# Two token-mixing stages reordered: turned blocks under the projection, gate sigmoids in the attention passes, results in pairs

## The chip, the cores and the metric

The program runs on one core of a Trainium2 chip. The metric is the time of one execution on the device in microseconds (us). The engines are TensorE (matrix products and transposes), VectorE, ScalarE, GpSimd and the DMA queues; each works through its own instructions in order, and they wait for each other by semaphores.

## The reference

The reference is two blocks one behind the other on 256 tokens of width 1024. The second block, where the change is, has two layers of feed-forward, token mixing, feed-forward. The mixing, cut to what matters:

```python
proj = n @ w_in                     # 3072 columns of q, k, v and small gates, then 3 x 1024 merge gates
y_a = _nsa_attention(...)           # 4 heads: compressed, selected, window
y_b = _dilated_attention(...)       # 3 groups of 2 heads, mixed by softmax over the groups' log-sum-exp
y_c = _forgetting_attention(...)    # 6 heads, bias cumsum(log_sigmoid(f_logit + f_bias))
g_a, g_b, g_c = jnp.split(jax.nn.sigmoid(merge_g), 3, axis=-1)
merged = g_a * (y_a @ br_nsa) + g_b * (y_b @ br_dil) + g_c * (y_c @ br_fox)
return merged @ w_out
```

## The kernel before, in words

All matrix products run in fp32 by three multiplications each: operands are split into a high part (fp32r) and the rest, and `mm3` (L353 to L355) multiplies high by high, low by high and high by low. Weights come in units of 128x2048 (1 MB) through a ring of three slots. For each unit ScalarE writes the high half (`conv_hi`, L274) once TensorE has used the unit three before, and VectorE then the low half (`conv_lo`, L280), at which TensorE may start; the queue of loads (L245) refills a slot when its low half is made. Where these conversions stand in the three engines' orders is written out by hand, and nothing is reordered by a planner.

A mixing stage (`pe_layer`, `act_layer`, `dve_layer`) has four parts. The projection is 12 units of 48 multiplications; ScalarE copies each result into `qj` (L1988). In layer 0 VectorE also does 16 steps of a modulation sum there (L320, L326), whose inputs share the load queue. In the second part come three of the twelve merge-gate units (`gate_unit`), the rotation of q and k (six VectorE instructions, L813 to L819), the forget gate's logarithm, 17 blocks of 128 columns turned by 34 transposes (L1851) and copied into `tb` by ScalarE (L2008) and VectorE (L2137) in turn, and the compression (two units of small multiplications). The third part is 20 attention passes of two query tiles each. In pass i TensorE makes the scores, turns the weights of pass i-1 and multiplies those of pass i-2 with v; VectorE takes the negated row maximum (L2229), ScalarE the exponentials with their sums (L2040) and a copy of the turned weights (L2051). Seven gate units (5 to 11) fill the gaps in halves: two passes of three have one, and in the third pass ScalarE copies the gate out and converts a unit, VectorE makes its low half. `oc_part` (L2201) is the compressed branch's output ahead of pass 0. In the fourth part the groups' weights are computed with a logarithm (L2054) and an exponential (L2056), the twelve gates get their sigmoid on ScalarE (L2060), outputs are normalised (L2261 to L2272) and turned (L421), split into halves (L469, L475), multiplied with the three branch matrices, gated (L2280), added (L2284), turned and split again, and multiplied with the output matrix.

Of the kernel before, what the change touches and what calls it, by code (L numbers as in the profile page):

```python
# [70 lines left out]
NTB = len(T_COLS)  # L71

# [51 lines left out]
def bass_network(nc, W, AD, x_in, ctx_in, s1_in, s2_in, k1_in, masks_in, gf_in, out):  # L124
    with ExitStack() as ctx:
# [1621 lines left out]
        def final_norm(dve, k, t, dst, done):  # L1747
# [8 lines left out]
                 "hid_made": 1, "ck_mm": 1, "ck_out": 1, "cs_mm": 1, "cs_sub": 1, "zeroed": 1, "hid_turned": 1, "hid_act": 1, "oc_out": 1, "sig_done": 3, "y_half": 1, "cs_exp": 1, "cs_done": 1, "cp_mm": 1,  # L1756
                 "cp_out": 1, "oc_mm": 1, "s2_mm": 20, "negmax2": 20, "exp2": 20, "p2_turned": 20, "pt2_out": 20, "pv2": 20,
                 "ya_done": 1, "den_ln": 1, "lse_sub": 1, "lse_exp": 1, "m_out": 12, "y2_turned": 7, "y2_hi": 7,
                 "y2_lo": 7, "dil_mm": 1, "br_out": 3, "y2_made": 1}
# [3 lines left out]
        ORDER2 = list(range(11, 17)) + list(range(11))  # L1763
# [15 lines left out]
        nsa_part = [tbf[:, 6 * S:8 * S], tbf[:, 8 * S:10 * S]]  # L1779
        dil_part = [tbf[:, b * S:b * S + S] for b in (2, 3, 4)]  # L1780
# [32 lines left out]
        def pe_layer(pe, l):  # L1813
# [12 lines left out]
            gate_pe(pe, N2, 1, l, 2)  # L1826
            for j in range(3, 12):
                pe.wait_ge(*B["q_out"].at(j - 3, l))
                project(unit(pe, QK0 + j, E0), hhi, hlo, QB[j % 3]).then_inc(unit_used, 1)
                if l == 0 and j in (6, 10):  # L1830
                    half_sum(pe, QKV_HALVES[j // 10], 3)
# [6 lines left out]

            gate_unit(0, 4)
            pe.wait_ge(*B["q_out"].at(11, l))  # L1840
            if l == 0:
                pe.wait_ge(*ada_out.at(QKV_HALVES[1] - PE_HALVES))
            pe.wait_ge(*N2.row.at(1, l))
            for i, b in enumerate(ORDER2):
                if i == 6:
                    gate_unit(1, 5)
                    pe.wait_ge(*B["rope2"].at(0, l))
                if i >= 4:
                    pe.wait_ge(*(B["tb_act"] if i % 2 == 0 else B["tb_dve"]).at(i // 2 - 2, l))
                for t in range(NT):  # L1850
                    ins = nc.tensor.transpose(PS[:, i % 4, t * P:(t + 1) * P], qj[:, t, T_COLS[b]:T_COLS[b] + P], ident)  # L1851
                ins.then_inc(*B["tb_mm"].up)
            gate_unit(2, 6)

# [15 lines left out]
            pe.wait_ge(*B["cum_out"].at(0, l))  # L1870
            for t in range(NT):
                ins = nc.tensor.transpose(PS[:, 3, (1 + t) * P:(2 + t) * P], ct[:, t], ident)
            ins.then_inc(*B["cum_turned"].up)
# [71 lines left out]
            pe.wait_ge(*B["y2_made"].at(0, l))  # L1945
            turn(pe, B["y2_turned"], xn, 0, 6)
            pe.wait_ge(*B["y2_lo"].at(2, l))

            u = unit(pe, BR0, E0)
            for kk in range(2):  # L1950
                ins = rows_product(u, kk, hhi[:, kk], hlo[:, kk], 4, kk == 0, kk == 1)
            ins.then_inc(unit_used, 1)
            u = unit(pe, BR0 + 1, E0)
            rows_product(u, 0, hhi[:, 2], hlo[:, 2], 0, True, True).then_inc(*B["dil_mm"].up)
            pe.wait_ge(*B["br_out"].at(0, l))
            rows_product(u, 1, hhi[:, 3], hlo[:, 3], 4, True, False).then_inc(unit_used, 1)
            u = unit(pe, BR0 + 2, E0)
            for kk in range(2):
                ins = rows_product(u, kk, hhi[:, 4 + kk], hlo[:, 4 + kk], 4, False, kk == 1)
            ins.then_inc(unit_used, 1)  # L1960
            pe.wait_ge(*B["br_out"].at(2, l))
            turn(pe, B["y2_turned"], mg, 0, DC)
# [11 lines left out]
        def act_layer(act, l):  # L1974
# [8 lines left out]
            norm_act(act, N2, 1, l, shift2(1, l), QK0, E0, x2_at(1, l))  # L1983
            for j in range(12):
                if j == 3:
                    gate_act(act, N2, 1, l, 2)
                act.wait_ge(unit_used, E0 * 3 + (QK0 + j + 1))
                nc.scalar.activation(qj[:, :, j * 256:j * 256 + 256], PS[:, QB[j % 3]].rearrange("p (t n) -> p t n", t=2),  # L1988
                                     ACT.Copy).then_inc(*B["q_out"].up)
                conv_hi(act, QK0 + j + RING, E0)  # L1990

            def gate_out(f, bank, conv=True):

                act.wait_ge(unit_used, E0 * 3 + (CG[f] + 1))
                nc.scalar.activation(G[f], PS[:, bank].rearrange("p (t n) -> p t n", t=2), ACT.Copy).then_inc(*B["m_out"].up)
                if conv:
                    conv_hi(act, CG[f] + RING, E0)

            act.wait_ge(*B["fox_abs"].at(0, l))
            nc.scalar.activation(ge.rearrange("p (t n) -> p t n", t=2), qj[:, :, C_G:C_F], ACT.Exp, scale=-1.0)  # L2000
            nc.scalar.activation(fe, fe, ACT.Exp, scale=-1.0)
            act.drain()
            nc.scalar.activation(fe, fe, ACT.Ln, bias=1.0).then_inc(*B["fox_ln"].up)
            def turned_out(a, b):
                for i in range(a, b, 2):
# [545 lines left out]
```

## Time and profile before

| | us |
|---|---|
| median of 3 runs | 2143.99 (2140.99 to 2145.86) |
| profiled execution, its own time | 2144.57 |
| its span, first to last instruction | 2142.8 |
| granted TensorE clock, mean | 0.949 of full |
| TensorE busy | 92% of the span |

The profile is of one execution. Layer 0's mixing stage begins its projection some 905 us behind the start, layer 1's some 727 us later. A multiplication's busy time overlaps with the next one's, so lengths of stretches are more telling than sums of durations.

### The profile page before, as it was taken

How to read it: one execution, taken by the hardware profiler on the slowest of the kernel's cores; microseconds unless marked ns; L12 is line 12 of the kernel's file. 1: busy time of each engine (PE TensorE's matmuls, PEld its weight loads, DVE VectorE, ACT ScalarE, POOL GpSimd, SP SyncE). 2: the span in 40 equal slices, each digit the busy share in tenths (PEclk: the TensorE clock that was granted, in tenths of full speed). 3: DMA queues.
4: the chain of work that ended last, by engine and by line, in shares of the span. 5: the costliest groups of instructions: out<-in, count | busy, mean ns of one | idle time of the engine just before them, and what ended most of it. 6: DMA issues, size and time to landing. Idle time of an engine off the chain costs nothing.

```text
span 2142.8 us, 29870 instructions
## 1 busy us (share of the span) xinstructions
PE 1964.4 (92%) x12658; PEld 1746.6 (82%) x12658; DVE 1377.5 (64%) x1467; ACT 997.1 (47%) x1161; POOL 82.3 (4%) x105
## 2 busy tenths in 40 slices
PE   7999879999997999997997899999999879879998
PEld 3977668888885999896875799989998877768997
DVE  4888558999995777664335587777755443355444
ACT  3344337777774433443444433343334434435342
POOL 1320000000001000000000000000001000000000
PEclk9988979999998999997998999999999989989999
DMA  8655328999994687553321387658753432124554
GB/s 347 238 210 185 156 109 334 367 357 350 349 376 173 256 299 262 224 217 107 109 79 71 146 325 293 266 190 335 292 185 139 176 118 79 67 91 158 178 194 149
DMA packets 63877, 458.42 MB, mean 214 GB/s; under 512 B 7040, under 2 KB 7296, under 8 KB 8832
## 3 DMA queue, kind: packets, MB, share of 16 engines
q1 hardware_dynamic: 63744, 456.51, 56.7%
q8 instruction: 100, 1.64, 0.3%
q14 instruction: 33, 0.27, 0.0%
HBM read 455.43 MB, written 1.05 MB: 213 GB/s over the span
## 4 chain that ended last, share of the span: by engine, by line
issue 80%; PE 7%; DVE 6%; DMA 3%; ACT 2%; POOL 1%; DVEq 1%; POOLq 0%; ACTq 0%; SPq 0%
DMA ada<-in_ada 2%; DVE acc L326 2%; PE PS L353 2%; PE PS L354 2%; PE PS L355 1%; DVE wlo L280 1%; PE PS L1194 1%; POOL Z L485 1%; ACT whi L274 1%; DVE hlo L462 1%; PE PS L1258 1%; DMA raw<-in_stream 0%; ACT Z L441 0%; PE PS L1270 0%; DVE sm L1702 0%
## 5 line engine op out<-in xcount | busy, mean ns | idle before, releaser
L280 DVE TENSOR_TENSOR wlo<-raw,whi 128x2048 fp32r<-128x2048 f32 x282 | 646.6, 2294 | 409.1 <-ACT whi L274 403.6
L274 ACT ACTIVATE whi<-raw 128x2048 fp32r<-128x2048 f32 x282 | 538.5, 1913 | 408.4 <-PE PS L355 364.1
L353 PE MATMUL PS<-whi,hhi 128*128 128x256 f32 (+1 forms) x1616 | 530.2, 328 | 39.7 <-DVE wlo L280 11.7
L354 PE MATMUL PS<-wlo,hhi 128*128 128x256 f32 (+1 forms) x1616 | 518.5, 321 | 0.0
L355 PE MATMUL PS<-whi,hlo 128*128 128x256 f32 (+1 forms) x1616 | 518.0, 321 | 0.0
L353 PEld LDWEIGHTS PS<-whi,hhi 128*128 128x128 f32 x1616 | 319.9, 198 | 65.8 <-issue 13.7
L355 PEld LDWEIGHTS PS<-whi,hlo 128*128 128x128 f32 x1616 | 319.6, 198 | 19.2
L354 PEld LDWEIGHTS PS<-wlo,hhi 128*128 128x128 f32 x1616 | 320.3, 198 | 17.6
L353 PE MATMUL PS<-hhi,whi 128*128 128x256 f32 x1152 | 326.6, 284 | 2.2 <-DVE mod L348 2.2
L355 PE MATMUL PS<-hhi,wlo 128*128 128x256 f32 x1152 | 326.0, 283 | 0.0
L354 PE MATMUL PS<-hlo,whi 128*128 128x256 f32 x1152 | 326.0, 283 | 0.0
L353 PE MATMUL PS<-whi,zr 128*128 128x512 f32 (+2 forms) x624 | 232.0, 375 | 13.9 <-DVE zr L2159 11.1
L326 DVE SCALAR_TENSOR_TENSOR acc<-ada,cs,acc 128x512 f32<-128x512 f32 x308 | 236.8, 769 | 8.9
L355 PE MATMUL PS<-whi,zr 128*128 128x512 f32 (+2 forms) x624 | 227.4, 367 | 0.0
L354 PE MATMUL PS<-wlo,zr 128*128 128x512 f32 (+2 forms) x624 | 227.1, 367 | 0.0
L353 PEld LDWEIGHTS PS<-hhi,whi 128*128 128x128 f32 x1152 | 221.0, 192 | 4.6 <-DVE mod L348 3.5
L354 PEld LDWEIGHTS PS<-hlo,whi 128*128 128x128 f32 x1152 | 221.0, 192 | 1.1
L355 PEld LDWEIGHTS PS<-hhi,wlo 128*128 128x128 f32 x1152 | 221.0, 192 | 0.0
L353 PEld LDWEIGHTS PS<-whi,zr 128*128 128x128 f32 (+1 forms) x624 | 113.7, 182 | 35.0 <-DVE zr L2159 11.2
L355 PEld LDWEIGHTS PS<-whi,zr 128*128 128x128 f32 (+1 forms) x624 | 113.5, 182 | 20.8
L354 PEld LDWEIGHTS PS<-wlo,zr 128*128 128x128 f32 (+1 forms) x624 | 113.7, 182 | 18.9
L280 DVE TENSOR_TENSOR wlo<-ada,whi 128x2048 fp32r<-128x2048 f32 x48 | 109.9, 2291 | 12.0 <-ACT whi L274 12.0
(377 smaller groups left out, 1822.0 us busy)
## 6 DMA issues: line engine op xcount, KB each, us to landing
raw<-in_stream SPq DMA_DIRECT2D x285, 1024.0 KB, 4.8
ada<-in_ada SPq DMA_DIRECT2D x92, 1024.0 KB, 4.9
ada<-in_stream SPq DMA_DIRECT2D x48, 1024.0 KB, 4.9
raw<-in_ada SPq DMA_DIRECT2D x3, 1024.0 KB, 15.5
xs<-in_x SPq DMA_DIRECT2D x1, 1024.0 KB, 11.7
Z<-in_ada SPq DMA_DIRECT2D x1, 1024.0 KB, 19.4
Z<-in_ctx SPq DMA_DIRECT2D x1, 1024.0 KB, 11.8
masks<-in_masks SPq DMA_DIRECT2D x2, 512.0 KB, 9.6
```

The costliest lines, as they stand in the source:

```text
L274: nc.scalar.activation(whi[:, s], src, ACT.Copy).then_inc(hi_ready, 1)
L280: nc.vector.tensor_tensor(wlo[:, s], src, whi[:, s].bitcast(F32), ALU.subtract).then_inc(lo_ready, 1)
L326: ins = nc.vector.scalar_tensor_tensor(a, w, c, a, ALU.mult, ALU.add)
L353: nc.tensor.matmul(out_, ah, bh, start=start, stop=False, skip_group_check=check)
L354: nc.tensor.matmul(out_, ah, bl, start=False, stop=False, skip_group_check=check)
L355: return nc.tensor.matmul(out_, al, bh, start=False, stop=stop, skip_group_check=check)
L462: nc.vector.tensor_tensor(lo[:, 4 * b:4 * b + 4, t * P:(t + 1) * P], ntmp[:, 4 * b:4 * b + 4], hi[:, 4 * b:4 * b + 4, t * P:(t + 1) * P].b ...
L485: nc.gpsimd.tensor_tensor(diag, mid(ident, [P, DC, P]), bc(gcol[:, :], [P, DC, P]), ALU.mult).then_inc(*N.diag.up)
L1194: ins = nc.tensor.matmul(PS[0:2, bank, :], cs[:, n:16:8], slot[:, 512 * k:512 * k + 512], start=n == 0, stop=n == 7)
L1258: ins = nc.tensor.matmul(PS[:, i % 2], q, k, start=True, stop=i >= 16, skip_group_check=i < 16)
```

## The change

In both layers: the last of the 12 projection units (small gates, values of the dilated group) goes first, so the forget gate is computed under the projection; the rotation follows VectorE's conversion of step 5; the 17 blocks are turned in five portions behind projection units 7 to 11, in an order that puts the compressed keys first, through result banks 2 to 5. `oc_part` goes ahead of a conversion. The merge gates are computed as 1/(1 + exp(-x)): gates 0 to 3 by an exponential in passes 0 to 3, gates 4 to 11 by one at their copy, then an addition and a reciprocal on VectorE; eleven of these fall in the passes, the twelfth behind. The groups' weights are computed from maxima and sums without a logarithm, in passes 15 to 18, and the outputs are normalised, turned and split in three pairs; the first two already beside the last passes. The halves of these pairs have places of their own (`zr`), and the branch products use other banks. The third branch's result is gated and merged in quarters, each turned as it is made. The products themselves, their number and the units' number stay the same; units are only reordered in the weight stream. Comment lines in the cut diff name the engine.

```diff
+QKV_ORDER = [11] + list(range(11))
+TURNS_AT = {7: (0, 4), 8: (4, 8), 9: (8, 12), 10: (12, 16), 11: (16, 17)}
...
-        ORDER2 = list(range(11, 17)) + list(range(11))
+        ORDER2 = [10, 8, 9, 6, 7, 0, 1, 2, 3, 4, 5] + list(range(11, 17))
...
# TensorE, pe_layer
+            def turn_blocks(a, b):
+                for i in range(a, b):
+                    if i >= 4:
+                        pe.wait_ge(*(B["tb_act"] if i % 2 == 0 else B["tb_dve"]).at(i // 2 - 2, l))
+                    for t in range(NT):
+                        c = T_COLS[ORDER2[i]]
+                        ins = nc.tensor.transpose(PS[:, 2 + i % 4, t * P:(t + 1) * P], qj[:, t, c:c + P], ident)
+                    ins.then_inc(*B["tb_mm"].up)
             for j in range(3, 12):
                 pe.wait_ge(*B["q_out"].at(j - 3, l))
                 project(unit(pe, QK0 + j, E0), hhi, hlo, QB[j % 3]).then_inc(unit_used, 1)
...
+                if j == 7:
+                    pe.wait_ge(*B["rope2"].at(0, l))
+                    pe.wait_ge(*N2.row.at(1, l))
+                if j in TURNS_AT:
+                    pe.wait_ge(*B["q_out"].at(j - 1, l))
+                    turn_blocks(*TURNS_AT[j])
...
             gate_unit(0, 4)
-            for i, b in enumerate(ORDER2):
-                if i == 6:
-                    gate_unit(1, 5)
-                    pe.wait_ge(*B["rope2"].at(0, l))
...
+            gate_unit(1, 5)
+            pe.wait_ge(*B["cum_out"].at(0, l))
+            for t in range(NT):
+                ins = nc.tensor.transpose(PS[:, 3, (1 + t) * P:(2 + t) * P], ct[:, t], ident)
+            gate_unit(2, 6)
...
+                if i == PASSES2:
+                    pe.wait_ge(*B["y2_made"].at(0, l))
+                    turn_two(xn, 0, 6)
+            pe.wait_ge(*B["y2_made"].at(1, l))
+            turn_two(xn, 2, 4)
+            pe.wait_ge(*B["y2_lo"].at(0, l))
+            rows_product(u, 0, yb_hi[:, 0], yb_lo[:, 0], 0, True, False)
+            pe.wait_ge(*B["y2_made"].at(2, l))
+            turn_two(xn, 4, 5)
+            rows_product(u, 1, yb_hi[:, 1], yb_lo[:, 1], 0, False, True).then_inc(unit_used, 1)
...
+            for j in range(4):
+                pe.wait_ge(*B["br_out"].at(2 + j, l))
+                turn_two(mg, 2 * j, 4 + j)
# ScalarE, act_layer: gate_out of units 4 and up writes exp(-x); in the passes
+                    if i < 4:
+                        nc.scalar.activation(G[i], G[i], ACT.Exp, scale=-1.0).then_inc(*B["gate_exp"].up)
+                    if i == 17:
+                        act.wait_ge(*B["lse_sub"].at(0, l))
+                        nc.scalar.activation(lw, lw, ACT.Exp).then_inc(*B["lse_exp"].up)
...
-            nc.scalar.activation(lnd, den2[:, 16:28], ACT.Ln).then_inc(*B["den_ln"].up)
-            for b in range(3):
-                for f in range(4 * b, 4 * b + 4):
-                    ins = nc.scalar.activation(G[f], G[f], ACT.Sigmoid)
# VectorE, dve_layer, under the projection
             for j in range(12):
                 conv_lo(dve, QK0 + j + RING, E0)
+                if j == 2:
+                    fox_start()
+                if j == 4:
+                    fox_log()
+                if j == 5:
+                    rotate()
...
                     half_step(dve, v, n)
                     half_step(dve, v, n + 1)
+                if j in TURNS_AT:
+                    turned_out(*TURNS_AT[j])
...
-            conv_lo(dve, CG[4] + RING, E0)
             nc.vector.tensor_tensor(oc_part...).then_inc(*B["oc_out"].up)
+            conv_lo(dve, CG[4] + RING, E0)
+            def gate_sigmoid(f):
+                dve.wait_ge(*(B["gate_exp"] if f < 4 else B["m_out"]).at(f, l))
+                nc.vector.tensor_scalar(G[f], G[f], 1.0, None, ALU.add)
+                dve.drain()
+                nc.vector.reciprocal(G[f], G[f])
...
                 if done[1]:
                     conv_lo(dve, CG[done[0]] + RING, E0)
+                    gate_sigmoid(done[0])
+                if i < 5:
+                    gate_sigmoid(i)
+                if i == 15:
+                    dil_weights()
+                if i == 18:
+                    dil_out()
+                if i == 19:
+                    fox_out(14, 2, 4, 256)
+            fox_out(16, 4, 5, 0)
+            split_lo(0, 6, yb_hi[:, 0:2], yb_lo[:, 0:2])
+            split_lo(1, 4, yb_hi[:, 2:4], yb_lo[:, 2:4])
+            split_lo(2, 5, yb_hi[:, 4:6], yb_lo[:, 4:6])
             conv_lo(dve, CG[11] + RING, E0)
+            gate_sigmoid(11)
...
+            for j in range(4):
+                ins = gated(0, j, 0, mg)
+            ins.then_inc(*B["br_out"].up)
             conv_lo(dve, BR0 + RING, E0)
+            for j in range(4):
+                gated(1, j, 4, mt2[0])
+            nc.vector.tensor_tensor(mg, mg, mt2[0], ALU.add).then_inc(*B["br_out"].up)
+            for j in range(2):
+                for t in range(NT):
+                    c = slice(256 * j, 256 * j + 256)
+                    nc.vector.tensor_tensor(mt2[1][:, t, c], PS[:, 2 * t, c], G[8 + j][:, t], ALU.mult)
+            merged(0)
+            gated(2, 2, 0, mt2[1])
+            merged(1)
+            gated(2, 3, 0, mt2[1])
+            merged(2)
+            merged(3)
+            for j in range(4):
+                split_lo(3 + j, 4 + j, hhi[:, 2 * j:2 * j + 2], hlo[:, 2 * j:2 * j + 2])
+            for u in range(1, 3):
+                conv_lo(dve, BR0 + u + RING, E0)
```

## Rows read from the trace of the kernel before

**Rows 1.** The page, part 1: busy us of each engine, share of the span, instructions.
```profile
PE 1964.4 (92%) x12658; PEld 1746.6 (82%) x12658; DVE 1377.5 (64%) x1467; ACT 997.1 (47%) x1161; POOL 82.3 (4%) x105
```

**Rows 2.** Stretches: length; busy us (instructions) of PE, PEld, DVE, ACT, POOL; clock, DMA, GB/s.
```profile
924.60:930.30 5.70, 5.70 (x50) 5.70 (x49) 3.05 (x3) 2.40 (x2) 0.00 (x0) 1.00 0.52 185
...
972.40:1023.70 51.30, 35.26 (x283) 34.06 (x281) 20.65 (x34) 18.45 (x24) 0.00 (x0) 0.77 0.28 101
...
1016.40:1020.80 4.40, 4.40 (x49) 4.40 (x50) 0.00 (x0) 0.00 (x0) 0.00 (x0) 0.61 0.58 227
...
1020.80:1023.70 2.90, 2.90 (x52) 2.90 (x49) 0.70 (x1) 1.91 (x1) 0.00 (x0) 1.00 0.00 0
...
1042.20:1142.20 100.00, 94.92 (x640) 79.00 (x640) 32.78 (x36) 40.89 (x114) 0.00 (x0) 0.97 0.22 74
...
1142.20:1185.30 43.10, 24.69 (x100) 20.12 (x100) 29.33 (x40) 21.03 (x28) 0.00 (x0) 0.80 0.24 86
...
1699.60:1750.80 51.20, 35.23 (x287) 34.03 (x286) 20.54 (x33) 18.45 (x24) 0.00 (x0) 0.77 0.28 103
```

**Rows 3.** Timeline of TensorE: start, us, instruction, count, [idle before, releaser].
```profile
978.20 1.03 PE L1851 MATMUL PS<-k,Z 128*128 128x128 f32 x8
...
984.62 0.69 PE L1851 MATMUL PS<-k,Z 128*128 128x128 f32 x2 [5.39 <-ACT Z L2008]
...
1000.35 2.82 PE L1851 MATMUL PS<-k,Z 128*128 128x128 f32 x12 [1.95 <-DVE Z L2137]
...
1016.39 0.32 PE L353 MATMUL PS<-whi,zr 128*32 128x128 f32 x1 [5.54 <-DVE zr L2159]
```

**Rows 4.** Timeline of ScalarE and VectorE in layer 0's projection, and the rotation.
```profile
944.03 1.91 ACT L274 ACTIVATE whi<-raw 128x2048 fp32r<-128x2048 f32 x1 [7.13 <-DMA raw<-in_stream]
...
945.98 2.29 DVE L280 TENSOR_TENSOR wlo<-raw,whi 128x2048 fp32r<-128x2048 f32 x1 [9.26 <-ACT whi L274]
...
977.35 0.48 DVE L813 TENSOR_TENSOR xn<-Z,k 128x320 f32<-128x320 f32 x1
...
979.52 0.49 DVE L819 TENSOR_TENSOR Z<-xn 128x320 f32<-128x320 f32 x1
```

**Rows 5.** Timeline of one block of three passes (a maximum comes first).
```profile
1069.74 0.69 DVE L2229 TENSOR_REDUCE sm<-PS 128x2 f32<-128x512 f32 x1 [5.38 <-PE PS L1915]
...
1072.13 1.93 ACT L274 ACTIVATE whi<-raw 128x2048 fp32r<-128x2048 f32 x1
...
1074.09 2.29 DVE L280 TENSOR_TENSOR wlo<-raw,whi 128x2048 fp32r<-128x2048 f32 x1 [3.65 <-ACT whi L274]
...
1076.30 0.69 DVE L2229 TENSOR_REDUCE sm<-PS 128x2 f32<-128x512 f32 x1
...
1077.98 0.55 PE L1924 MATMUL PS<-k,ada 128*128 128x128 f32 x3 [0.80 <-ACT ada L2040]
```

**Rows 6.** VectorE's instructions by line and shape: count, busy us, mean ns.
```profile
L320 DVE TENSOR_SCALAR acc<-ada,cs 128x512 f32<-128x512 f32 x44 | 23.0, 523 | 11.0 <-DMA ada<-in_ada 11.0
...
L2219 DVE TENSOR_TENSOR Z<-Z 128x512 f32<-128x512 f32 x2 | 1.4, 693 | 0.2
...
L2129 DVE RECIPROCAL sm<-sm 128x24 f32<-128x24 f32 x2 | 0.6, 303 | 0.1
...
L2192 DVE RECIPROCAL acc<-acc 128x8 f32<-128x8 f32 x2 | 0.4, 204 | 0.1
...
L1169 DVE RECIPROCAL sm<-sm 128x2 f32<-128x2 f32 x1 | 0.2, 168 | 0.1
```

**Rows 7.** Timeline behind the passes, TensorE and VectorE.
```profile
1150.73 2.82 PE L421 MATMUL PS<-k,xn 128*128 128x128 f32 x12 [8.56 <-DVE xn L2272]
...
1163.88 2.48 DVE L2280 TENSOR_TENSOR Z<-PS,Z 128x512 f32<-128x512 f32 x4 [7.32 <-PE PS L355]
...
1171.03 2.29 DVE L2284 TENSOR_TENSOR Z<-Z,ada 128x2048 f32<-128x2048 f32 x1
...
1180.34 3.57 PE L421 MATMUL PS<-k,Z 128*128 128x128 f32 x16 [5.43 <-DVE Z L2284]
```

More of the change, by code:

```diff
@@ L1944, in pe_layer @@
                     gate_unit(f, 7, tile)
[L1945 to L1946 removed]
+                if i == PASSES2:
[4 more added lines that the diff above has]
+            pe.wait_ge(*B["y2_lo"].at(0, l))
+            u = unit(pe, BR0, E0)
+            rows_product(u, 0, yb_hi[:, 0], yb_lo[:, 0], 0, True, False)
@@ L1955, in pe_layer @@
             pe.wait_ge(*B["br_out"].at(0, l))
-            rows_product(u, 1, hhi[:, 3], hlo[:, 3], 4, True, False).then_inc(unit_used, 1)
+            rows_product(u, 1, yb_hi[:, 3], yb_lo[:, 3], 0, True, False).then_inc(unit_used, 1)
             u = unit(pe, BR0 + 2, E0)
[L1958 to L1962, printed above, removed]
+            rows_product(u, 0, yb_hi[:, 4], yb_lo[:, 4], 0, False, False)
@@ new lines, in pe_layer @@
+            wh, wl = (w.rearrange("p (k n) -> p k n", k=2)[:, 1] for w in u)
+            for half in range(2):
+                for t in range(NT):
+                    o, w = slice(t * P, (t + 1) * P), slice(half * 512, half * 512 + 512)
+                    ins = mm3(PS[:, 2 * t + half], yb_hi[:, 5, o], yb_lo[:, 5, o], wh[:, w], wl[:, w], False, True)
+                ins.then_inc(*(unit_used, 1) if half else B["dil_mm"].up)
+            for j in range(4):
+                pe.wait_ge(*B["br_out"].at(2 + j, l))
+                turn_two(mg, 2 * j, 4 + j)
@@ L1999, in act_layer @@
[L1999 to L2005, printed above, removed]
-                    act.wait_ge(*B["tb_mm"].at(i, l))
-                    k = ORDER2[i]
-                    nc.scalar.activation(tb[:, k], PS[:, i % 4, 0:256], ACT.Copy,
-                                         scale=HD ** -0.5 if k in T_SCALED else 1.0).then_inc(*B["tb_act"].up)
@@ L2012, in act_layer @@
-            conv_hi(act, CG[0] + RING, E0)
-            turned_out(0, 6)
-            conv_hi(act, CG[1] + RING, E0)
-            turned_out(6, NTB)
-            for f in range(2):
-                gate_out(f, 4 + f, False)
-            gate_out(2, 6)
+                if j == 3:
+                    act.wait_ge(*B["fox_abs"].at(0, l))
+                    nc.scalar.activation(ge.rearrange("p (t n) -> p t n", t=2), qj[:, :, C_G:C_F], ACT.Exp, scale=-1.0)
+                    nc.scalar.activation(fe, fe, ACT.Exp, scale=-1.0)
+                    act.drain()
+                    nc.scalar.activation(fe, fe, ACT.Ln, bias=1.0).then_inc(*B["fox_ln"].up)
@@ L2296, in dve_layer, with merged @@
-            split_dve(dve, B["y2_hi"], B["y2_lo"], 3, 4, l)
+            for j in range(4):
+                gated(1, j, 4, mt2[0])
+            dve.drain()
+            nc.vector.tensor_tensor(mg, mg, mt2[0], ALU.add).then_inc(*B["br_out"].up)
+            dve.wait_ge(*B["dil_mm"].at(1, l))
+            def merged(j):
+                c = slice(256 * j, 256 * j + 256)
+                nc.vector.tensor_tensor(mg[:, :, c], mg[:, :, c], mt2[1][:, :, c], ALU.add).then_inc(*B["br_out"].up)
+            for j in range(2):
+                for t in range(NT):
+                    c = slice(256 * j, 256 * j + 256)
+                    nc.vector.tensor_tensor(mt2[1][:, t, c], PS[:, 2 * t, c], G[8 + j][:, t], ALU.mult)
@@ L2297, in dve_layer @@
+            dve.drain()
+            merged(0)
+            dve.wait_ge(unit_used, E0 * 3 + (BR0 + 3))
+            gated(2, 2, 0, mt2[1])
+            merged(1)
+            gated(2, 3, 0, mt2[1])
+            dve.drain()
+            merged(2)
+            merged(3)
+            for j in range(4):
+                split_lo(3 + j, 4 + j, hhi[:, 2 * j:2 * j + 2], hlo[:, 2 * j:2 * j + 2])
+            for u in range(1, 3):
+                conv_lo(dve, BR0 + u + RING, E0)
             conv_lo(dve, WO0 + RING, E0)
```

259 lines of the change are left out of this document (137 added, 122 removed).

## The prediction

> **What bounds the kernel now.** I read the shares of the engines first: TensorE is busy for 1964 of 2143 us, VectorE for 64%, ScalarE for 47% [rows 1]. So in most stretches a change is worth what it does to TensorE's queue, and only idle or slow-clock TensorE time can be won. The table by stretches shows where that is in a mixing stage. In the projection TensorE never rests: 50 multiplications take 5.7 us, so a unit of 48 takes about 5.8. The 51.3 us behind it (first gate unit, turns, compression) hold only 35 us of TensorE work, at a mean granted clock of 0.77 of full; the 43.1 us behind the passes hold 25, at 0.80. The 100 us of passes are 95% busy. The other layer repeats this to 0.1 us [rows 2]. In the turns TensorE stands still for 5.4 us until the last projected unit has been copied and rotated, later again, the last time for 2.0 us, and for 5.5 us ahead of the compression [rows 3]. Behind the passes it waits 8.6 us for weights, mixing and turning inputs, and 5.4 us for the merged result [rows 7]. All of that is what the change attacks. What it gives away lies in the passes.
>
> **Turns under the projection: a gain of 22.9 us per layer.** Old: 51.3 us [rows 2]. New: 34 turns (8 take some 0.9 us net [rows 3]) 4.1 us; three gate units at 5.8, 17.4 us; two compression units at 2.9 us, as the one at full clock took [rows 2], 5.8 us; the small products and the turned sums 1.1 us. Sum 28.4, gain 22.9. It needs each operand early. The units' low halves follow a unit's end by 0.6 + 1.9 + 2.3 = 4.8 us and are wanted 11.5 us behind it; ScalarE does 0.6 + 1.9 + 2 x 0.4 and VectorE 2.3 + 2 x 0.4 us per unit of 6.7, so both keep up. The forget gate's exponentials and logarithm fall in one such unit, where ScalarE's 3.3 us leave as much idle. At the compression the operand (ready about 11.5 us behind the start of the first gate unit) is long there when TensorE comes to it at 18.4. What is late behind it, the activation of the hidden row, keeps its order and its delay.
>
> **Layer 0 gives back 5.7 us.** There VectorE also does 16 steps of modulation, and a weight unit lands late: its conversion starts at 944.03 after a wait of 7.1 us on the DMA, and its low half ends at 948.27 [rows 4], with a quarter of a us to spare before TensorE's next unit. The transfer waits for the modulation step behind which the change puts the 0.8 us of the forget gate, so it lands later by 0.8. Then come the low half (949.1) and the six rotation instructions, 2.7 us from 977.35 to 980.01 [rows 4], now ahead of everything: the first turns wait until 951.9, 2.3 to 3.4 us behind the place where TensorE is ready; the modulation steps behind them (1.5 us each unit) make VectorE's first copy late too, at 961.5, so the next turns wait 2.5 us (or the slow clock of the first wait takes the same time). Together 5.7. Without this queue in layer 1: nothing.
>
> **Gates in the passes: the price of a reciprocal.** Twelve sigmoids on ScalarE behind the passes become exponentials there plus, on VectorE, an addition (about 0.5 us, as the 128x512 instruction with a factor, mean 523 ns [rows 6]) and a reciprocal over 128x512. The trace has none of that size. Its bounds: an ordinary instruction of 512 elements, 0.69 us; and the slope of the small reciprocals, 168 ns for 2 elements, 204 for 8, 303 for 24 [rows 6]: (303 - 168)/22 = 6.1 ns per element, so 0.16 + 512 x 6.1 = 3.3 us. The slope is even over all sizes, while ordinary instructions cost (2290 - 693)/1536 = 1.04 ns [rows 4, 6]. I take 3.3; with the addition and the drain between, a gate costs VectorE 3.86 us. The upper bound is eight ordinary passes per element, 8 x 1.04 x 512 = 4.3 us.
>
> The Trainium skill, VectorE: DVE Perf Modes, under "First, the fixed hardware budget", says that a reciprocal is an iterative divide with a repeat count of 8. The trace agrees in kind, at six ordinary elements' time rather than eight. It speaks against this change; by eight, each sigmoid would cost 1 us more, and that case is a rival below.
>
> Is VectorE's time hidden? It has 67 idle us in the 100 [rows 2], and 11 sigmoids are 42 us: yes by the share, no by the order. A block of three passes takes 13.6 us. Its chain: maximum at 1069.74, exponentials, gate copy, copy of the turned block, conversion on ScalarE from 1072.13, low half on VectorE from 1074.09, and only then the next pass's maximum at 1076.30, whose exponential TensorE awaits for 0.8 us already [rows 5]. So there is no slack: the sigmoid of 3.86 us goes between low half and maximum, and the whole of it is TensorE's wait, 0.8 becoming 4.7 us. Four blocks (maxima of passes 9, 12, 15, 18) give 4 x 3.86 = 15.4 us. The first two blocks carry five more sigmoids. I walk them: oc_part now ends at 1042.95, conversion 1045.3, maximum 0 1046.0, gate exponential 0.6 and pass 0.9, sigmoid 0 until 1050.5, maximum 1 1051.2, sigmoid 1 until 1055.7, maximum 2 1056.4, exponentials and the three ScalarE pieces until 1061.0, low half 1063.3, sigmoids 5 and 2 until 1071.0, exponential 3 ready at 1073.3 (before: 1064.4). The same walk through sigmoids 3, 4 and 6 gives exponential 6 at 1093.3 instead of 1077.9: +15.4 us. The 1.9 us that oc_part wins by going ahead of a conversion are inside that. Sum 30.8 us per layer. The dilated group's weights and outputs (3 us at passes 15 and 18) lie beside gate work or in the last wait.
>
> To this comes the clock. A wait of 5.5 us left the clock at 1.2 GHz: 49 multiplications in 4.4 us where 52 then took 2.9 [rows 2, 3], so a wait costs some 1.5 us again. The 0.8 us waits of the passes leave it full (0.97 [rows 2]). Five to six waits of 4.7 to 9.5 us, and TensorE's next gate half is in the chain: 7.5 us (bounds 0 and 12). The Trainium skill, TensorE: Matmul & The Clock Gate, in "Part 1", says that the throttled state is the default and activity releases it; this agrees with those rows. Passes: +38.3 us per layer.
>
> **Behind the passes: a gain of 10.7 us per layer.** Removed: logarithm, two table loads, all but one sigmoid, the dilated mixing. New, from the last pass's end (0): last outputs 1.05, low half of the first pair 2.4, first product (12 multiplications of 512, 2.8 us) to 5.1, turn, second to 8.4, third to 11.2. VectorE meanwhile: low halves to 7.0, conversion 9.3, last sigmoid 13.2, four gated products of 2.48 us in all [rows 7] 15.7. TensorE waits for these 4.5 us and runs on partly at the slow clock: 19.8, 22.6, 25.4. VectorE: conversion, second branch 2.48, addition 2.29 [rows 7] to 22.9, then four halves and the merging in quarters to 29.8, four low halves 32.4. The output product starts at 32.4 instead of 43.1. The splitting into pairs helps little, because VectorE is last at every step.
>
> **The sum.** Per layer -22.9 + 38.3 - 10.7 = +4.7; two layers +9.4; with layer 0's 5.7, +15.1 us. The profiled execution took 2144.57 us (span 2142.8), 0.6 above the median 2143.99; 2144.6 + 15.1 = 2159.7, against the median 2159.
>
> **The rivals.**
> Cheap reciprocal (faster). If the 512-element reciprocal costs like any other, 0.69 us, a gate costs 1.25 us, the passes +7 us (+14 if the 2.1 us waits slow the clock), the tail gains 13.5: per layer -29 to -22, in all 2092 to 2106, say 2100. It decides from where a reciprocal is under about 2.6 us: at 3.86 us for a gate the change loses 4.7 a layer, each 0.1 us less returns 1.1. For it: no large reciprocal is in the trace. Against it: five sizes on one line. 0.17.
> Clock stays up (no change). Waits of 4.7 us broken by multiplications don't bring the clock down: 7.5 us and 1.4 in the tail back per layer, 2142. For it: the waits are shorter than the 5.5 us that brought it down, and multiplications stand between them. Against: the first stretch behind the passes, at 0.80 with waits of that size. 0.14.
> The turns stall the projection in both layers (slower). Each of the five stops waits 2.0 us for copies, as the last turns did before [rows 3], +10 us a layer: 2159.7 + 20 = 2180. Against: each copy has a unit of 5.8 us. 0.07.
> Eight passes per element (slower): +1 us per sigmoid, eleven in the chain, 2183. 0.05.
>
> **How the numbers follow.** My forecast has 0.57, with a range of its own of 2143 to 2177 (clock 0 to 12, walk within 3 us a layer, layer 0's wait 2 to 9). What this measurement can tell is 0.2%, 4.3 us. Slower: 0.57 x 0.92 + 0.12 = 0.64. Same: 0.57 x 0.05 + 0.14 x 0.6 = 0.11. Faster: the rest, 0.25. The range goes from 2110, which leaves out most of the cheap reciprocal, to 2180.
>
> **What would show it.** The row of the reciprocal over 128x512 on VectorE, at 3.3 us or not: it decides most. TensorE's wait ahead of the turned blocks in the passes, 4.7 us instead of 0.8, some six times a layer, and the clock there; the stretch of passes at 138 us instead of 100. Gate unit 0 to the second compression unit in 24 us, with no wait of over 1 us. In layer 0 a wait of 2 to 3 us on the rotation. From the passes' end to the output product 32 us, with VectorE last. I am wrong if the passes stay within 115 us, or if the front's 22.9 us turn up as waits in the projection.

## The result, and the profile after

The changed kernel takes 2154.51 us (median of five runs, 2153.53 to 2156.53) against 2143.95 (2140.99 to 2145.86) for the kernel before: ratio 1.0051, 95% interval [1.0037, 1.0065]. It is slower by 10.6 us; 2159 was predicted. The profiled spans are 2154.8 and 2142.8 us. Here the differences are told by stage, cut at the same events in both traces (us, after minus before; layer 0 and layer 1):

```
stage                                        before        after         difference     predicted
projection to end of compression         104.8, 102.4   86.0,  79.4   -18.8, -23.0   -17.2, -22.9
compression to first scores               18.3,  18.3   18.3,  18.3     0.0,   0.0
passes, to the last value product        100.0,  99.9  139.9, 136.4   +39.9, +36.5   +38.3
behind them, to the output product        43.2,  43.1   32.9,  32.9   -10.3, -10.2   -10.7
```

They sum to +14.1 us; 2.1 us less stand outside the mixing stages, which makes the 12.0 of the spans. The page of after, part 1, answers to [rows 1]: VectorE has 86 us more, TensorE 12 more with the same instructions.

```profile
PE 1976.2 (92%) x12658; PEld 1758.8 (82%) x12658; DVE 1463.1 (68%) x1525; ACT 978.9 (45%) x1137; POOL 82.8 (4%) x105
```

The stretches of after (columns as in [rows 2]): front, passes and tail of layer 0, then of layer 1.

```profile
918.25:1004.27 86.02, 83.13 (x731) 82.68 (x731) 53.65 (x63) 39.10 (x42) 2.93 (x5) 0.98 0.52 191
1022.56:1162.42 139.86, 112.30 (x647) 96.49 (x647) 75.87 (x71) 43.03 (x119) 0.00 (x0) 0.82 0.15 53
1162.42:1195.31 32.89, 22.91 (x96) 17.42 (x95) 25.77 (x33) 9.71 (x11) 0.00 (x0) 0.90 0.18 64
1658.63:1738.05 79.42, 79.42 (x716) 79.41 (x715) 43.10 (x45) 38.77 (x42) 0.00 (x0) 1.00 0.50 180
1756.35:1892.71 136.36, 109.16 (x647) 93.21 (x647) 75.90 (x71) 43.03 (x119) 0.00 (x0) 0.85 0.16 55
1892.71:1925.65 32.94, 22.96 (x96) 17.49 (x94) 25.77 (x33) 9.71 (x11) 0.00 (x0) 0.90 0.18 64
```

Read three things. In layer 1 the front is pure TensorE work: 79.42 busy of 79.42 us at clock 1.00, where the turns had left holes. In the passes TensorE is idle for 27.6 us (139.86 - 112.30) instead of 5.1 [rows 2], and its same work costs 17.4 us more (112.30 against 94.92), since the granted clock is 0.82 instead of 0.97 (of the 17.4, some 0.6 us are the first pair's transposes, which now stand in this stretch). And VectorE has more than twice the work, 75.9 us instead of 32.8.

VectorE's groups by shape show the price (count, busy us, mean ns, idle before). The reciprocal costs the 3.3 us that the small sizes of [rows 6] gave on one line (16 of the 24 instructions of each kind are in this group; the other groups' means are within 6 ns of these):

```profile
L2287 DVE RECIPROCAL Z<-Z 128x512 f32<-128x512 f32 x16 | 53.6, 3353 | 1.2
...
L2285 DVE TENSOR_SCALAR Z<-Z 128x512 f32<-128x512 f32 x16 | 6.6, 414 | 4.2 <-ACT Z L2073 4.2
```

A block of three passes, from the timeline of VectorE and ScalarE, answers to [rows 5]. Between the low half (1083.91) and the next maximum there was nothing before; now addition and reciprocal stand there, and the exponential waits for the maximum behind them:

```profile
1083.91 2.29 DVE L282 TENSOR_TENSOR wlo<-raw,whi 128x2048 fp32r<-128x2048 f32 x1 [3.65 <-ACT whi L276]
1086.11 0.42 DVE L2285 TENSOR_SCALAR Z<-Z 128x512 f32<-128x512 f32 x1
...
1086.61 3.35 DVE L2287 RECIPROCAL Z<-Z 128x512 f32<-128x512 f32 x1
1089.88 1.22 DVE L2333 TENSOR_REDUCE sm<-PS 128x2 f32<-128x512 f32 x2
1090.54 0.37 ACT L2080 ACTIVATE ada<-PS,sm 128x128 f32<-128x128 f32 x1 [6.67 <-DVE sm L2333]
```

The turned blocks are the three transposes of a pass's weights, which TensorE can start only when the pass's exponentials are made. Those of passes 3, 6, 9, 12, 15 and 18 in layer 0 (timeline, idle time before and its releaser in brackets):

```profile
1052.76 0.90 PE L1942 MATMUL PS<-k,ada 128*128 128x128 f32 x3 [7.21 <-ACT ada L2080]
...
1071.88 0.90 PE L1942 MATMUL PS<-k,ada 128*128 128x128 f32 x3 [4.50 <-ACT ada L2080]
...
1091.51 0.90 PE L1942 MATMUL PS<-k,ada 128*128 128x128 f32 x3 [4.50 <-ACT ada L2080]
...
1111.87 0.90 PE L1942 MATMUL PS<-k,ada 128*128 128x128 f32 x3 [4.86 <-ACT ada L2080]
...
1132.96 0.90 PE L1942 MATMUL PS<-k,ada 128*128 128x128 f32 x3 [2.64 <-ACT ada L2080]
...
1153.89 0.90 PE L1942 MATMUL PS<-k,ada 128*128 128x128 f32 x3 [2.73 <-ACT ada L2080]
```

Each takes 0.90 us where the same block took 0.55 before [rows 5]. The three stretches from the second of them on (columns as above) show why: a clock of 0.50 and 0.62, that is mostly the 1.2 GHz level, for 6.6 us behind the wait, then full again.

```profile
1071.88:1073.70 1.82, 1.82 (x9) 1.82 (x10) 0.00 (x0) 1.51 (x6) 0.00 (x0) 0.50 0.00 0
1073.70:1078.50 4.80, 4.80 (x27) 4.64 (x26) 0.00 (x0) 0.00 (x0) 0.00 (x0) 0.62 0.00 0
1078.50:1087.40 8.90, 8.51 (x57) 6.61 (x56) 4.11 (x4) 3.58 (x7) 0.00 (x0) 1.00 0.06 9
```

The same wait doesn't always slow the clock as much. Layer 1 has the same six waits within 0.4 us, but at passes 15 and 18 its turned blocks still take 0.55 us, and the clock falls later and for a shorter time. Pass 15, its block and the two stretches behind the wait (in layer 0 the first 5.5 us behind this wait were at 0.50):

```profile
1865.10 0.55 PE L1942 MATMUL PS<-k,ada 128*128 128x128 f32 x3 [2.64 <-ACT ada L2080]
```

```profile
1865.10:1867.00 1.90, 1.90 (x11) 1.83 (x12) 0.11 (x1) 1.51 (x6) 0.00 (x0) 0.70 0.00 0
1867.00:1872.80 5.80, 5.80 (x33) 4.89 (x31) 0.00 (x0) 0.00 (x0) 0.00 (x0) 0.80 0.00 0
```

### The profile page after: what moved, and what is told of

It reads as the page before. It is cut to its first block, busy times and chain, and to the rows that moved or that the text cites. A ratio compares the mean times of both kernels' runs of the same rounds, so it can differ in the third digit from the quotient of the medians.

```text
span 2154.8 us, 29942 instructions
## 1 busy us (share of the span) xinstructions
PE 1976.2 (92%) x12658; PEld 1758.8 (82%) x12658; DVE 1463.1 (68%) x1525; ACT 978.9 (45%) x1137; POOL 82.8 (4%) x105
## 4 chain that ended last, share of the span: by engine, by line
issue 80%; DVE 6%; PE 6%; DMA 3%; ACT 2%; POOL 1%; DVEq 1%; POOLq 0%; ACTq 0%; SPq 0%
DMA ada<-in_ada 2%; DVE acc L328 2%; DVE wlo L282 2%; PE PS L355 1%; PE PS L356 1%; PE PS L357 1%; ACT whi L276 1%; DMA raw<-in_stream 1%; PE PS L1196 1%; POOL Z L487 1%; DVE hlo L464 1%; PE PS L1260 0%; ACT Z L443 0%; DVE acc L322 0%; DVE Z L459 0%
## 5 line engine op out<-in xcount | busy, mean ns | idle before, releaser
L355 PE MATMUL PS<-whi,hhi 128*128 128x256 f32 (+1 forms) x1568 | 517.7, 330 | 30.9 <-DVE wlo L282 11.9
L356 PE MATMUL PS<-wlo,hhi 128*128 128x256 f32 (+1 forms) x1568 | 504.8, 322 | 0.0
L357 PE MATMUL PS<-whi,hlo 128*128 128x256 f32 (+1 forms) x1568 | 504.1, 321 | 0.0
L355 PE MATMUL PS<-whi,zr 128*128 128x512 f32 (+2 forms) x672 | 250.9, 377 | 15.0 <-DVE Z L2364 8.9
L357 PE MATMUL PS<-whi,zr 128*128 128x512 f32 (+2 forms) x672 | 245.6, 369 | 0.0
L356 PE MATMUL PS<-wlo,zr 128*128 128x512 f32 (+2 forms) x672 | 245.2, 369 | 0.0
L355 PEld LDWEIGHTS PS<-whi,zr 128*128 128x128 f32 (+1 forms) x672 | 122.8, 183 | 39.3 <-DVE Z L2364 9.7
L357 PEld LDWEIGHTS PS<-whi,zr 128*128 128x128 f32 (+1 forms) x672 | 122.4, 182 | 23.3
L356 PEld LDWEIGHTS PS<-wlo,zr 128*128 128x128 f32 (+1 forms) x672 | 122.7, 183 | 21.1
```

The source lines that it names most:

```text
L355: nc.tensor.matmul(out_, ah, bh, start=start, stop=False, skip_group_check=check)
L356: nc.tensor.matmul(out_, ah, bl, start=False, stop=False, skip_group_check=check)
L357: return nc.tensor.matmul(out_, al, bh, start=False, stop=stop, skip_group_check=check)
```

## The experiments

All start from the kernel after unless another is named; ratios are against the kernel before, from the same chip. "Passes" and "tail" are the third and fourth stage of the table, layer 0 and layer 1. The recorded expectations end the passes a little earlier, so the kernel after reads 138.6 and 135.9 us there, and its tails 34.2 and 33.4, where the table has 139.9 and 136.4, and 32.9 twice.

**Without the reciprocal.**

This leaves out the reciprocal, so the gates are wrong. The exponential's factor is made small as well, which keeps them near 2.

```diff
-nc.scalar.activation(G[f], src, ACT.Exp, scale=-1.0)
+nc.scalar.activation(G[f], src, ACT.Exp, scale=-0.001)
...
 def gate_sigmoid(f):
     nc.vector.tensor_scalar(G[f], G[f], 1.0, None, ALU.add)
-    dve.drain()
-    nc.vector.reciprocal(G[f], G[f])
```

> The kernel after, with the reciprocal (and the drain ahead of it) left out of the twelve gate units, so that the gates are 1 + exp(-0.001 x) and not the sigmoid; the addition of 0.42 us, the exponentials and the order of all work stay. Theory (the 3.35 us reciprocal stands between the low half of the gate weights and the next row maximum, and the passes wait for it): the passes of attention fall from 138.6 and 135.9 us back to 102 to 107, the 4.5 us waits of TensorE ahead of every third pass go, its clock stays up, and the whole comes to 2080 to 2092 us. Rival (the exponentials and copies of ScalarE, or a TensorE clock that falls for another reason, stretch the passes): passes stay over 120 us and the whole over 2120. Rival (VectorE catches up behind the passes): passes 105, but the tail grows by over 5 us per layer.

Measured: 2076.63 us, ratio 0.970 [0.969, 0.972]; passes 103.1 and 103.1, tail 28.6 and 28.6, front unchanged. The passes are as the theory said, the whole is 3 us below its range, and both rivals are refuted: this one instruction costs the change some 78 us, 35 of them in each layer's passes and 4.3 in each tail.

**The gate as a hyperbolic tangent.**

```diff
-nc.scalar.activation(G[f], src, ACT.Exp, scale=-1.0)
+nc.scalar.activation(G[f], src, ACT.Tanh, scale=0.5)
...
-nc.vector.tensor_scalar(G[f], G[f], 1.0, None, ALU.add)
-dve.drain()
-nc.vector.reciprocal(G[f], G[f])
+nc.vector.tensor_scalar(G[f], G[f], 0.5, 0.5, ALU.mult, ALU.add)
```

> The kernel after with the gate as 0.5 tanh(x/2) + 0.5: ScalarE computes Tanh where it computed Exp, VectorE one multiply-and-add in place of addition, drain and reciprocal. Theory as for the kernel without reciprocals: VectorE's 3.86 us per gate become about 0.42, passes 102 to 107 us, whole 2080 to 2095 us if Tanh costs what Exp does and no table is loaded between it and the exponentials. Rival (each Tanh between two Exp of the passes loads a table twice, over 1 us each): 11 gate units per layer add two loads, 20 us or more per layer, whole over 2120 us. The Trainium skill, ScalarE: Activation LUTs (Table sets: the hidden batching unit), puts exp and tanh into one set; no run here has shown it so far, and this one does.

Measured: 2078.18 us, ratio 0.970 [0.969, 0.972]; passes 103.0 and 103.0, tail 27.4 and 27.4; the whole is 2 us below the theory's range. No table load stands among the exponentials and hyperbolic tangents of the passes. The Trainium skill (ScalarE: Activation LUTs, Table sets: the hidden batching unit) puts exp and tanh into one set, and this run agrees. ScalarE's Tanh over 128x512 takes 592 to 631 ns (means of its groups), and VectorE's groups show the block shrunk from 3.86 us for addition, drain and reciprocal to 0.42 us:

```profile
L2285 DVE TENSOR_SCALAR Z<-Z 128x512 f32<-128x512 f32 x16 | 6.6, 423 | 4.2 <-ACT Z L2073 4.2
```

**The same sigmoids at other places.**

```diff
+SIGMOIDS_AT = {1: (0,), 3: (1,), 4: (2,), 6: (3,), 7: (4,), 9: (5,), 10: (6,), 13: (7,), 15: (8,), 16: (9,), 19: (10,)}
...
-                    gate_sigmoid(done[0])
-                if i < 5:
-                    gate_sigmoid(i)
+                for f in SIGMOIDS_AT.get(i, ()):
+                    gate_sigmoid(f)
```

> The kernel after with the same eleven sigmoids inside the passes, each put off to a place behind the row maximum of a pass whose filler is a gate half, or behind the last fillers: behind the maxima of passes 1, 3, 4, 6, 7, 9, 10, 13, 15, 16 and 19 in place of 0 to 4, 3, 6, 9, 12, 15 and 18. Nothing is left out. Theory that the order costs the time, not the share of VectorE (it is busy 76 of 138.6 us): one reciprocal of 3.35 us fits beside the 3.1 us gate half, the passes come to 103 to 115 us and the whole to 2090 to 2115. Rival (a block of 3.86 us ahead of any maximum costs nearly itself, as a pass has only two score banks): passes stay at 130 or more and the whole within 10 us of 2154.5.

Measured: 2093.37 us, ratio 0.977 [0.976, 0.979]; passes 103.7 and 103.6, tail 34.9 and 33.8. The stretch of the passes:

```profile
1023.96:1127.65 103.69, 98.87 (x645) 82.73 (x644) 75.19 (x70) 43.35 (x119) 0.00 (x0) 0.93 0.19 72
```

VectorE works 75.2 us as in after, but the stretch is 36 us shorter than layer 0's in after, and TensorE is idle for 4.8 us. So the order was the matter and not the share of VectorE. The eleven blocks of 3.86 us cost 3.7 us over the kernel before when they stand behind a maximum that TensorE follows with a gate half, and 39.9 and 36.5 us, waits and slower clock together, when they stand ahead of the next maximum. Some 2 and 1 us of the gain come back in the tails.

**The clock held up.**

```diff
+FILLS = {3: 52, 15: 20, 18: 20}
...
                     p = i - 1
+                    if p % 3 == 0 and 3 <= p <= 18:
+                        for n in range(FILLS.get(p, 32)):
+                            nc.tensor.matmul(PS[:, 7, 256:512], zb[:, 0:P], zb[:, 0:256], start=True, stop=True)
                     pe.wait_ge(*B["exp2"].at(p, l))
```

> The kernel after with 20 to 52 multiplications of 128x256 (bf16, their result unused, into a free half of a bank) put into each of TensorE's six waits ahead of the turned blocks of passes 3, 6, 9, 12, 15 and 18; all that is computed stays. Theory (7.5 us per layer of the passes are TensorE at its lower clock behind these waits, where a gate half takes 4.1 to 5.2 us in place of 3.1): the gate halves return to 3.1 us, the passes fall by 5 to 8 us per layer and the whole to 2138 to 2146. Rival (VectorE sets the pace of the passes, and TensorE's slower blocks lie in its shadow): under 2 us per layer, 2150 to 2155. Rival (the added multiplications overrun the waits and the clock stays low all the same): 2155 or more.

Measured: 2136.18 us, ratio 0.997 [0.996, 0.998], 18 us under after and even under the kernel before; passes 127.3 and 126.3. The theory's direction holds and its size is too small: the passes are 12.6 and 10.1 us shorter. Both rivals are refuted. The stretches of the passes, both layers:

```profile
1023.89:1151.20 127.31, 120.11 (x835) 100.82 (x835) 75.91 (x71) 43.03 (x119) 0.00 (x0) 0.95 0.16 59
1746.96:1873.27 126.31, 117.41 (x835) 97.86 (x835) 75.76 (x71) 43.06 (x119) 0.00 (x0) 0.97 0.17 59
```

All of VectorE's blocks are still there (75.9 us). So of the 39.9 and 36.5 us at least 12.6 and 10.1 were the clock. The tail of layer 0 is 1.9 us longer than in after (34.8 us): behind its first wait of 1.6 us the clock is at 0.64 for 4.7 us, where after has 1.00.

**The reciprocal kept for units 0 to 4 only**, tanh for 5 to 11 (both edits as above, by `f > 4`).

> The kernel after with the reciprocal kept for gate units 0 to 4 (five blocks of 3.86 us in passes 0 to 4) and 0.5 tanh(x/2) + 0.5 for units 5 to 11. Nothing is left out. Theory (a block costs only where it stands between the low half and the next maximum while nothing is queued on TensorE; in passes 0 to 2 the gate halves of 3.1 us cover most of it, and only pass 3 has a pile of two): passes 106 to 113 us, whole 2085 to 2100. Rival (each of the eleven blocks costs its share of the 36 us alike, five of them 16): passes 118 to 120, whole 2105 to 2112.

Measured: 2086.26 us, ratio 0.974 [0.973, 0.976]; passes 109.1 and 107.4, tail 27.4 and 28.6. Five blocks with the reciprocal cost 6.1 and 4.4 us over the 103.0 of the tanh kernel, which has none, and the eleven cost 36.9 and 33.4: not alike, and the theory holds. (In layer 0, 1.5 of the 6.1 us stand ahead of the first turned block, where TensorE doesn't wait and its clock is lower than in the tanh kernel; a slower clock is part of the price here too.) TensorE's timeline at the turned blocks of passes 3 and 6 shows the pile at the place expected, and little behind it; in after the same two waits were 7.21 and 4.50 us:

```profile
1046.71 0.55 PE L1942 MATMUL PS<-k,ada 128*128 128x128 f32 x3 [3.83 <-ACT ada L2082]
...
1062.47 0.55 PE L1942 MATMUL PS<-k,ada 128*128 128x128 f32 x3 [1.14 <-ACT ada L2082]
```

**Sigmoids behind the passes**, as before the change, with the rest of the change kept.

```diff
-                    ins = nc.scalar.activation(G[f], src, ACT.Exp, scale=-1.0)
+                    ins = nc.scalar.activation(G[f], src, ACT.Copy)
...
-                    gate_sigmoid(done[0])
-                if i < 5:
-                    gate_sigmoid(i)
...
             split_hi(2, 5, yb_hi[:, 4:6])
+            for b in range(3):
+                for f in range(4 * b, 4 * b + 4):
+                    ins = nc.scalar.activation(G[f], G[f], ACT.Sigmoid)
+                ins.then_inc(*B["sig_done"].up)
```

> The kernel after with the gates as in the kernel before: the units are copied as they are, and ScalarE applies Sigmoid to all twelve behind the passes (after the first parts of y are taken out), so that no gate work stands on VectorE in the passes. The turns under the projection, the weights without logarithm, the results in pairs and the new order of the last products stay. Nothing is left out. Theory (all that the change lost is the gate units' place): passes 101 to 104 us, tail 34 to 40 us (twelve Sigmoid of some 0.6 us and a table load in each direction stand ahead of the gated products), front 86.0 and 79.4 us as in after, whole 2088 to 2100 us. Rival (the tail's gain was the sigmoids' and goes with them): tail 43 us or more, whole over 2104.

Measured: 2076.60 us, ratio 0.970 [0.969, 0.971]; passes 98.9 and 98.9, tail 30.8 and 30.8. It comes out better than the theory's numbers: passes 1 us under those before, and a tail 12.3 us shorter although all twelve sigmoids are back in it. ScalarE's timeline there shows why they cost so little:

```profile
1124.71 0.60 ACT L2091 ACTIVATE zr<-PS 128x512 fp32r<-128x512 f32 x1 [3.78 <-PE PS L1864]
1125.33 1.28 ACT L2098 ACT_TABLE_LOAD   x1
1126.62 4.28 ACT L2098 ACTIVATE Z<-Z 128x512 f32<-128x512 f32 x8
```

They run mostly beside TensorE's products of the first branch (1121.2 to 1130.2). So everything in the change but the gates' place and form is worth about 66 us.

**The rotation ahead of its low half.**

```diff
             for j in range(12):
+                if j == 5:
+                    rotate()
                 conv_lo(dve, QK0 + j + RING, E0)
...
-                if j == 4:
+                if j == 4 and l:
                     fox_log()
-                if j == 5:
-                    rotate()
...
                     half_step(dve, v, n + 1)
+                if j == 4 and not l:
+                    fox_log()
```

> The kernel after with the rotation ahead of the low half of its turn in both layers, and, in layer 0, the logarithm's end behind the half steps. Nothing is left out. Theory (in layer 0 TensorE's 2.68 us wait ahead of the first turns under the projection, and the clock at its lower level that follows over unit 8, come from the rotation that stands behind VectorE's half steps): layer 0's part up to the compression falls by 2.7 to 6 us, the whole to 2149 to 2152. Rival (the wait is for q_out or the ring and not for the rotation): no change, 2154 to 2155.

Measured: 2152.90 us, ratio 1.006 [1.004, 1.008], 0.9 us above the theory's range; front of layer 0 82.9 instead of 86.0 us, span 2151.6 instead of 2154.8. By the timed medians the step of 1.6 us is within the noise; the stage in the trace shows the 3.1 us. The wait in after that it removes:

```profile
950.60 1.54 PE L1837 MATMUL PS<-k,Z 128*128 128x128 f32 x8 [2.68 <-DVE Z L821]
```

**Both of the last kind together**, tanh and rotation.

> The kernel after with the gates as 0.5 tanh(x/2) + 0.5 and with the rotation ahead of the low half of its turn, layer 0's logarithm behind the half steps. Nothing is left out. Theory (the two gains stand in different stages and add): front of layer 0 82.9 us, passes 103 us, whole 2074 to 2076 us, 1.5 to 3.5 under the kernel with the tanh alone. Rival (clock or DMA takes the 3.1 us back later): within 1 us of 2078.

Measured: 2075.17 us, ratio 0.969 [0.967, 0.970]; front of layer 0 83.0, passes 102.8 and 103.1, tail 28.6 and 28.6. 3.0 us under tanh alone, as the theory said. In the tails 1.2 us each go back, and the clock takes them. Both kernels wait 1.63 us ahead of the first branch's product; behind the wait the clock stays full in the tanh kernel and falls here, in both layers. What decides this the runs don't show. First the tanh kernel, then this one (layer 0):

```profile
1128.65:1132.50 3.85, 3.85 (x19) 3.17 (x20) 0.55 (x1) 0.31 (x1) 0.00 (x0) 1.00 0.02 4
```

```profile
1122.00:1126.00 4.00, 4.00 (x11) 3.13 (x12) 0.54 (x1) 0.00 (x0) 0.00 (x0) 0.57 0.01 4
```

**The last sigmoid behind the second branch.**

```diff
-            gate_sigmoid(11)
...
             nc.vector.tensor_tensor(mg, mg, mt2[0], ALU.add).then_inc(*B["br_out"].up)
+            gate_sigmoid(11)
             dve.wait_ge(*B["dil_mm"].at(1, l))
```

> The kernel after with the last gate's sigmoid (unit 11, 3.86 us on VectorE) moved behind the sum of the first two gated branches, where VectorE waits 2.7 us for TensorE; nothing is left out. Theory (the prediction's tail was short of its gain because this block stands ahead of the first gated products, and TensorE waits 4.44 us there, in the trace from 1173.45 to 1177.90, with a lower clock behind it): the tail falls from 34.2 and 33.4 us to 29 to 31, passes unchanged at 138.6 and 135.9, whole 2144 to 2149. Rival (the products of the second branch are bound by their weights' low half or by the ring, not by the gated products): tail over 33, whole 2152 to 2155.

Measured: 2156.64 us, ratio 1.006 [1.004, 1.007]: no gain. The passes stay at some 140 and 137 us. The tail does fall, to 30.4 and 30.4, but the wait has only moved. It now stands ahead of the last turns (4.30 us, where after waits 0.92), and the clock falls over the output product: the same 48 multiplications take 13.2 us instead of 11.2. First the wait (layer 0), then the output product in this kernel and in after (layer 1):

```profile
1186.23 2.31 PE L1864 MATMUL PS<-k,Z 128*128 128x128 f32 x8 [4.30 <-DVE Z L2382]
```

```profile
1922.26:1935.47 13.21, 13.21 (x49) 10.76 (x50) 6.89 (x5) 2.94 (x2) 0.00 (x0) 0.83 0.45 164
```

```profile
1925.65:1936.85 11.20, 11.20 (x49) 9.28 (x50) 6.89 (x5) 2.62 (x2) 0.00 (x0) 1.00 0.52 193
```

A group of 24 multiplications some 30 us later takes 4.64 instead of 3.15 us, behind a wait of 2.2 us that both kernels have. The two make 3.5 us, and that is all of the lead with which this kernel came to the output product (1922.26 against 1925.65). The theory was right on the wait's cause and wrong on what its removal brings; the rival's tail of over 33 us didn't come, though the whole did, for another reason than it named.

**No gate work on VectorE**, on top of tanh and rotation.

```diff
-nc.vector.tensor_tensor(dst[...], PS[...], G[4 * b + j], ALU.mult)
+nc.vector.scalar_tensor_tensor(dst[...], G[4 * b + j], 1.0, PS[...], ALU.add, ALU.mult)
...
 # splits of the turned sum: the factor 0.5
-nc.scalar.activation(hi, PS[:, bank], ACT.Copy)
-nc.vector.tensor_tensor(lo, PS[:, bank], hi, ALU.subtract)
+nc.scalar.activation(hi, PS[:, bank], ACT.Copy, scale=0.5)
+nc.vector.scalar_tensor_tensor(lo, PS[:, bank], 0.5, hi, ALU.mult, ALU.subtract)
```

> The kernel with tanh and the earlier rotation, with no gate work on VectorE at all: the gated product is (tanh(x/2) + 1) times the branch in one instruction, the factor 0.5 goes into the splits of the turned sum, and units 0 to 3 get their Tanh behind the passes, on ScalarE while it is idle. Nothing is left out. Theory (what the tanh kernel still pays over the 98.9 us of the passes without gate work is the 0.42 us pieces and ScalarE's four early Tanh, whose waits the trace of that kernel puts at 5.4 us of TensorE): passes 98.5 to 99.5 us, tail 27.5 to 29.5, whole 2065 to 2070 us. Rival (the Tanh pieces behind the passes delay the first gated product as twelve Sigmoid did, and the fused products are slower): tail 31 or more, whole 2072 to 2076.

Measured: 2066.64 us, ratio 0.964 [0.962, 0.965], the fastest of all: 76.5 us under the kernel before on the same chip. Passes 98.9 and 98.9, tail 27.0 and 26.7. The passes and the whole are in the theory's ranges; the tails are 0.5 and 0.8 us below theirs.

```profile
1019.21:1118.09 98.88, 94.13 (x637) 79.72 (x647) 36.17 (x49) 41.01 (x115) 0.00 (x0) 0.97 0.21 75
1118.09:1145.08 26.99, 21.01 (x97) 16.18 (x94) 22.16 (x31) 11.46 (x15) 0.00 (x0) 0.94 0.22 78
```

## Why the prediction was right, and where its terms were off

**The turns under the projection** were worked out to 0.1 us in layer 1 (-23.0 against -22.9).

**Layer 0's give-back** was put at 5.7 us and is 4.2 (23.0 - 18.8). The wait on the rotation is there, 2.68 us where 2.3 to 3.4 was said, and the earlier rotation wins 3.1. The second term was 2.5 us, as a wait at the next turns or as slow clock. It was the slow clock, and smaller: the wait is 0.21, the projected unit behind the first wait takes 7.2 us (951.8 to 959.0) instead of 5.8.

**The reciprocal**, taken at 3.3 us from three sizes of at most 24 elements, is 3.353. The addition was taken at 0.5 and is 0.42. This carried the verdict: without the reciprocal the kernel runs at 2077, 65 us under the kernel before. The rival of the cheap reciprocal had said 2100, with 0.69 us for it and not nothing.

**The waits in the passes** are the mis-sized term. Predicted 30.8 us more per layer; TensorE's idle time grew by 22.5 us (27.6 against 5.1). Two causes, both in the rows. The four later blocks were priced alike at 0.8 + 3.86: the first two of them are (4.50, 4.86), but at passes 15 and 18 the waits are 2.64 and 2.73. The trace before has its 0.8 us waits at passes 3, 6, 9 and 12 only and none at those two; from pass 14 on each pass's scores have more multiplications, which is the likely reason and was not tried. I had read one block and multiplied. And the walk over the first two blocks gave 15.4, while the waits at passes 3 and 6 come to 11.7, of which 1.6 were there before.

**The clock** was put at 7.5 us with bounds of 0 and 12, and it is above the upper bound: TensorE's busy time over nearly the same work grew by 17.4 us in layer 0 and 14.3 in layer 1, and the multiplications put into the waits gave back 12.6 and 10.1. The price of 1.5 us per wait was taken from one stretch of 4.4 us; the fall lasts up to some 6.6 us behind a wait here, and the next multiplications start every 0.21 us instead of every 0.12. From a turned block to the next pass's, layer 0 takes 1.8 us more than before at pass 3 and 2.4 to 2.8 at the other five (pass 6: 7.58 instead of 5.19 us); layer 1 takes 1.8, 2.4 and 2.8 at the first three and 1.5 to 1.6 at the last three. In layer 0 the waits of 2.6 us bring the clock down like those of 4.5, in layer 1 for a shorter time; passes 12, 15 and 18 make up the 3.1 us between the two layers. So the length of a wait doesn't fix its price in clock: in the tanh kernel a wait of 1.99 us at pass 3 is followed by a granted clock of 0.50 and 0.61, in the kernel with the first five reciprocals one of 3.83 us at the same place by 0.62 and 0.79. The sum of the two terms, 38.3, stands against 39.9 and 36.5 only because their errors cancel; that the forecast came so close is luck in these two terms. The filled kernel's clock is 0.95 and 0.97 instead of 0.82 and 0.85. The Trainium skill (TensorE: Matmul & The Clock Gate, Part 1) says that the throttled state is the default and activity releases it; the filled kernel agrees.

**Behind the passes**: -10.3 and -10.2 against -10.7. TensorE's wait for the gated products is 4.44 us (4.5 said), in the place that was said, and VectorE is last at each later step.

**The rivals.** The clock did not stay up. The turns do not stall the projection in layer 1 (clock 1.00, idle 0). Eight ordinary passes per element are refuted by 3353 ns, 6.2 ns per element besides the fixed part. The Trainium skill (VectorE: DVE Perf Modes, First, the fixed hardware budget) gives the reciprocal a repeat count of 8 and no time; taken as eight ordinary elements' time the count is too high here, where it is six.

## What to carry to other kernels

An engine with 67 idle us in 100 can't take 42 us of work at just any place. Find the one instruction on it that the bound engine's next step waits for, and put long work behind it, beside a filler, never ahead of it: the same eleven blocks cost 36 to 40 us a layer or 4 by place alone. Price a wait on TensorE as the wait and the slow clock behind it (here 1.5 to 2.8 us, not the same each time), and read every block before multiplying one. Where a sigmoid must go beside exponentials, 0.5 tanh(x/2) + 0.5 from ScalarE needs neither a reciprocal nor, in these runs, a table load.

## What the runs showed of the hardware

- A reciprocal over 128x512 takes 3353 ns on VectorE, five times the 0.69 us of an ordinary two-operand instruction of that size; Tanh on ScalarE takes 592 to 631 ns, and none of the passes' exponentials reloads a table for it. The load for Sigmoid takes 1.28 us.
- In layer 0, waits of 2.64 and 2.73 us in the middle of multiplications were followed by 5 us and more at the 1.2 GHz level, where turned blocks take 0.90 us instead of 0.55; in layer 1 the same waits left the blocks at 0.55 and cost 1 us less each. A wait of 1.63 us left the clock full in one kernel and at 0.57 for 4 us in another. Throwaway bf16 multiplications in such waits made the kernel 18 us faster.
- A wait of 4.4 us that was moved by 13 us, with no work added, gained nothing in the whole: it stood at its new place with 4.30 us, and the product behind it ran at clock 0.83 instead of 1.00.
